# A two-layer hybrid decoder: column tiles that take in a new input together, one table for eight PSUM banks, residual adds on VectorE

## The reference

```python
hn = _rmsnorm(h, g_mix_pre) * valid
u = hn @ w_in                      # 1024 -> 7704 columns, feeds four token mixers and the merge gates
y_sb, y_gla, y_ml, y_ret = ...     # stick-breaking attention, GLA, mLSTM, retention; 256 wide each
merged = sum_n sigmoid(merge_n + b_n) * (y_n @ w_branch[n])
h = h + _rmsnorm(merged @ w_out, g_mix_post)
f = _rmsnorm(h, g_ffn_pre)
h = h + _rmsnorm((silu(f @ ffn_w_gate) * (f @ ffn_w_up)) @ ffn_w_down, g_ffn_post)
```

## Time and profile before

| | |
|---|---|
| median of 3 runs | 1026.15 us (1025.69 to 1026.33) |
| the profiled execution | 1025.4 us |
| its span in the profile | 1023.6 us, 19877 instructions |
| mean granted TensorE clock | 0.992 of full speed |
| HBM read | 154.50 MB, 152 GB/s over the span |
| weights cut on VectorE (L1282) | 355.3 us busy, x290 |
| weights cut on ScalarE (L976) | 302.0 us busy, x290 |

### The profile page before, as it was taken

The page is one execution under the profiler, slowest core; times in us unless marked ns, Lnnn a source line. Parts: engine busy times, 40 slices in busy tenths (PEclk is TensorE's granted clock), DMA queues, the critical chain, the costliest instruction groups (busy, mean ns, idle before and its releaser), DMA issues.

```text
span 1023.6 us, 19877 instructions
## 1 busy us (share of the span) xinstructions
PE 998.8 (98%) x7744; PEld 941.0 (92%) x7744; DVE 600.5 (59%) x843; ACT 518.1 (51%) x825; POOL 152.1 (15%) x140
## 2 busy tenths in 40 slices
PE   7999999999999999999989999999999999999998
PEld 5999888899997999999969998888999899999996
DVE  8556564357956555554465565743679466656443
ACT  5443754465466444544345537544755555454442
POOL 2000000002623121210030000000034321222011
PEclk8999999999999999999999999999999999999998
DMA  5864433335562555555526543343465535555551
GB/s 157 281 214 147 132 94 124 116 109 147 170 195 74 179 164 167 180 176 185 150 67 198 173 142 112 119 124 124 125 165 165 164 124 180 189 180 189 186 185 41
DMA packets 168521, 156.40 MB, mean 153 GB/s; under 512 B 9091, under 2 KB 167022, under 8 KB 168078
## 3 DMA queue, kind: packets, MB, share of 16 engines
q1 hardware_dynamic: 167598, 152.13, 47.9%
q10 hardware_dynamic: 672, 3.37, 1.0%
q0 software_dynamic: 192, 0.07, 0.0%
HBM read 154.50 MB, written 1.05 MB: 152 GB/s over the span
## 4 chain that ended last, share of the span: by engine, by line
PE 88%; DVE 7%; ACT 2%; DMA 2%; issue 1%; SPq 1%; ACTq 0%; DVEq 0%
PE banks L588 27%; PE banks L590 26%; PE banks L589 26%; DVE sub L1300 2%; DMA raw<-in_w_in 2%; DVE sq L1291 1%; PE banks L801 1%; PE banks L803 1%; PE banks L613 1%; DVE lo L1282 1%; ACT hi L976 1%; PE banks L829 1%; PE banks L837 1%; DVE xl L1315 0%; PE banks L767 0%
## 5 line engine op out<-in xcount | busy, mean ns | idle before, releaser
L588 PE MATMUL banks<-xh,hi 128*128 128x272 f32 (+1 forms) x1680 | 490.9, 292 | 9.7 <-DVE xl L1315 4.8
L590 PE MATMUL banks<-xh,lo 128*128 128x272 f32 (+1 forms) x1680 | 480.9, 286 | 0.0
L589 PE MATMUL banks<-xl,hi 128*128 128x272 f32 (+1 forms) x1680 | 479.4, 285 | 0.0
L1282 DVE TENSOR_TENSOR lo<-raw,hi 128x1024 fp32r<-128x1024 f32 (+1 forms) x290 | 355.3, 1228 | 175.1 <-ACT hi L976 173.9
L976 ACT ACTIVATE hi<-raw 128x1024 fp32r<-128x1024 f32 (+1 forms) x290 | 302.0, 1042 | 95.4 <-PE banks L590 55.0
L588 PEld LDWEIGHTS banks<-xh,hi 128*128 128x128 f32 x1680 | 316.4, 188 | 22.8 <-issue 7.8
L589 PEld LDWEIGHTS banks<-xl,hi 128*128 128x128 f32 x1680 | 316.4, 188 | 0.9
L590 PEld LDWEIGHTS banks<-xh,lo 128*128 128x128 f32 x1680 | 316.6, 188 | 0.0
L1664 POOL TENSOR_TENSOR half<-term 128x544 f32<-128x544 f32 (+1 forms) x14 | 31.3, 2238 | 467.9 <-DVE term L1537 467.9
L590 PE MATMUL banks<-ah,lo 128*128 128x272 f32 (+1 forms) x352 | 100.4, 285 | 0.0
L588 PE MATMUL banks<-ah,hi 128*128 128x272 f32 (+1 forms) x352 | 100.1, 284 | 0.0
(11 more groups left out here) (238 smaller groups left out, 1101.7 us busy)
## 6 DMA issues: line engine op xcount, KB each, us to landing
raw<-in_w_in SPq DMA_DIRECT2D x54, 1024.0 KB, 5.2
raw<-in_ffn_w_gate SPq DMA_DIRECT2D x22, 1024.0 KB, 5.3
raw<-in_ffn_w_up SPq DMA_DIRECT2D x22, 1024.0 KB, 5.3
raw<-in_ffn_w_down SPq DMA_DIRECT2D x16, 1024.0 KB, 4.9
raw<-in_w_out SPq DMA_DIRECT2D x8, 1024.0 KB, 5.0
raw<-in_w_in SPq DMA_DIRECT2D x12, 512.0 KB, 4.4
raw<-in_w_branch SPq DMA_DIRECT2D x12, 512.0 KB, 5.5
raw<-in_ffn_w_down SPq DMA_DIRECT2D x8, 768.0 KB, 4.2
```

The source lines that it names most:

```text
L588: mm(dst, wh, mh, start=start, stop=False)
L589: mm(dst, wh, ml, start=False, stop=False)
L590: return mm(dst, wl, mh, start=False, stop=stop)
L1282: tt(lo[g % 2][:, 0:k, c:c + P], raw[g % 2][:, 0:k, c:c + P], hi[g % 2][:, 0:k, c:c + P].bitcast(F32), ALU.subtract).then_inc(lo_ready, 2 ...
```

## The change

- **Together.** A new `together` walks two or three column tiles over the k-tiles in an order given as a list of (tile, k-tile), each tile in a bank of its own; what a k-tile needs (`high_ready`, `low_ready`) is waited for once, the high part before the first matmul and the low part before the third. It is used for `small` and both tiles of `mqk0` (step `first`; lags in k-tiles between them 0, 3, 6 in layer 0 and 0, 0, 3 in layer 1), for the first two tiles of `output` (k-tiles 0 to 5 of both, then 6 and 7), and for the first three of `gate_up`, with the mean of norm 2 beside them.
- **Banks.** `plan_tiles` gives each tile a bank out of eight and a use number (`PLACE`); `bank_free` has one semaphore for each bank. The mixer's tiles still turn between two banks; `output`, `gate_up` and `down` turn in four. The loop of `output` is written out.
- **No dummy matmuls** but the four at the start.
- **VectorE alone** adds the sub-layers (`add_sublayer`: multiply by rstd, add to `hT`, and behind norm 1 `xl`, interleaved by k-tile); the gain is applied by ScalarE in `take_sublayer`. VectorE also makes all of `xl` in `pre_norm`, interleaved with the scaled k-tiles, and in layer 0 with the low parts of halves 0, 2 and 3; half 4 follows.
- **Weights earlier.** The halves of group `mqk1` change places (`SWAPPED`), so its first half lies where `small` has no columns and needn't wait for it. `gate` goes behind `mqk1`. In layer 1, half 3 is cut before the squares and before `pre_norm`; the fourth half of `gate_up` is cut on VectorE within `add_sublayer`. `root(l, 1)` goes ahead of a `round_half` on ScalarE.
- **Start.** ScalarE squares x by tokens with a running sum (`square_first`), right after x has landed and beside the transposes, scales an identity by the sums, and TensorE spreads them over the partitions with three matmuls (`mean_square_first`).

The core of the diff:

```diff
-WARM_START, WARM_PRE, WARM_POST = 4, 6, 8
+RING, NORM_BANK = (0, 1, 2, 3), 5
+FIRST_BANKS, MQK1_BANKS, FFN_BANKS, OUT_BANKS = (0, 1, 7), (4, 0), (4, 6, 7, 3), (4, 6, 7, 1)
+FIRST_LAGS = ((0, 3, 6), (0, 0, 3))
+OUT_ORDER = [(n, k) for n in range(2) for k in range(KT - 2)] + [(n, k) for k in (KT - 2, KT - 1) for n in range(2)]
...
+            def together(tiles, order, mh, ml, q0, high_ready, low_ready, beside=None):
+                open_at, seen = {}, -1
+                for n, k in order:
+                    t, g, c = tiles[n]
+                    if k == 0:
+                        open_at[n] = use_half(g, c), open_tile(t)
+                    (wh, wl), ps = open_at[n]
+                    f, dst = half_cols(g, c), ps[:, 0:T - q0]
+                    if k > seen:
+                        high_ready(k)
+                    mm(dst, wh[:, k, f], mh[:, k, q0:], start=k == 0, stop=False)
+                    mm(dst, wl[:, k, f], mh[:, k, q0:], start=False, stop=False)
+                    if k > seen:
+                        low_ready(k)
+                    last = mm(dst, wh[:, k, f], ml[:, k, q0:], start=False, stop=k == KT - 1)
...
             def output(l):
-                with pe.Fori(0, NOUT // 2) as i:
-                    for j in range(2):
-                        for c in range(2):
-                            features(t + 2 * j + c, g + j, c, gathered_h, gathered_l, q0, i, 2, merged_ready if j + c == 0 else None)
+                together([(t, g, 0), (t + 1, g, 1)], OUT_ORDER, gathered_h, gathered_l, q0, ...)
+                pe.wait_ge(branch_free[l], 2 * KT)
+                for m in range(2, KT):
+                    features(t + m, g + m // 2, m % 2, gathered_h, gathered_l, q0)
             def gate_up(l):
+                together([(t, g, 0), (t + 1, g, 1), (t + 2, g + 1, 0)], in_step((0, 0, 0)), xh, xl, q0, ..., mean_square(l, 2, q0))
+                features(t + 3, g + 1, 1, xh, xl, q0)
...
-                keep_warm(WARM_PRE)
-                pe.wait_ge(branch_free[l], 2 * KT)
-                keep_warm(WARM_POST)
-                keep_warm(WARM_POST - 1)
...
+            def square_first():
+                ss, spare = sq[:, KT - 1, 0:3], (sub[:, 0:4, 0:256], sub[:, 4:8, 0:256])
+                act.wait_ge(meta_loaded, 16)
+                fn(spare[0][0:META], xt[0:META, 0, :]..., ACT.Square, accum_out=ss[0:META, 0:1]).then_inc(ss_ready, 1)
+                act.wait_ge(x_loaded[0], 16)
+                act.wait_ge(x_loaded[1], 16)
+                for b in range(1, 3):
+                    fn(spare[b % 2], xt[:, b, :]..., ACT.Square, accum_out=ss[:, b:b + 1]).then_inc(ss_ready, 1)
+                for b, n in enumerate((META, P, P)):
+                    fn(sq[0:n, b, 0:n], cut["ident"][0:n, 0:n], ACT.Copy, scale=ss[0:n, b:b + 1]).then_inc(ss_ready, 1)
...
             def pre_norm(l):
+                for k in range(KT + 1):
+                    if k < KT:
+                        stt(sq[:, k, :], hT[:, k, :], par[...], rstd[:], ALU.mult, ALU.mult).then_inc(xn_ready[l], 1)
+                    if l == 0 and k == 1:
+                        rest_of_half(0)
+                    if k:
+                        dve.wait_ge(xh_ready[l], k)
+                        tt(xl[:, k - 1, :], sq[:, k - 1, :], xh[:, k - 1, :].bitcast(F32), ALU.subtract).then_inc(xl_ready[l], 1)
+                    if l == 0 and k in (2, 5):
+                        rest_of_half(k // 2 + 1)
+                rest_of_half(2 * G_MIX[l] + ROUND_AHEAD)
+            def add_sublayer(l, n, q0, behind=None):
+                dve.wait_ge(rstd_ready[l], n + 1)
+                for k in range(KT + 2):
+                    if k < KT:
+                        tt(sub[:, k, q0:], sub[:, k, q0:], rstd[:, q0:], ALU.mult).then_inc(post_scaled[l], 1)
+                    if 0 < k <= KT:
+                        dve.wait_ge(post_scaled[l], n // 2 * KT + k)
+                        tt(hT[:, k - 1, q0:], hT[:, k - 1, q0:], sub[:, k - 1, q0:], ALU.add).then_inc(h_ready[l], 1)
+                    if k > 1 and behind:
+                        behind(k - 2)
...
             def gate_up(l):    # VectorE, in the loop
+                    for c in range(2):
+                        dve.wait_ge(al_ready[l], c + 1 + i * 2)
+                        gate_tile(c, t + 4 + c, i, 4)
```

More of the change, by code:

```diff
@@ L21 @@
+import itertools
 from contextlib import ExitStack
@@ L254, in last_of @@
         signal.append(("half", halves, used))
-    free(KT + DEPTH)
+        put(bank)
+    free(*RING, *RING, *RING[:DEPTH])
     for _ in range(DEPTH):
         f = {}
+        turn = itertools.cycle(RING[:2])
         def stage(name):
             f[name] = len(signal)
-        stage("norm0"), free(1)
+        stage("norm0"), free(NORM_BANK)
         for step in STEPS:
             stage(step)
-            if step[0] == "group":
-                kind = KIND[step[1]]
-                if kind == "two":
-                    last_of(1), last_of(1)
-                else:
-                    last_of(2)
+            if step[0] == "first":
+                stage(("group", "small")), last_of(FIRST_BANKS[0], 2)
+                stage(("group", "mqk0")), [last_of(bank) for bank in FIRST_BANKS[1:]]
+            elif step == ("group", "mqk1"):
+                [last_of(bank) for bank in MQK1_BANKS]
+                next(turn)
+            elif step[0] == "group":
+                last_of(next(turn)), last_of(next(turn))
             elif step[0] == "logit":
-                last_of(1)
+                last_of(next(turn))
             elif step[0] == "branch":
@@ L445, in build, with half_cols @@
         G_END = GROUPS * DEPTH
+        SWAPPED = [g + MIX_NO["mqk1"] for g in G_MIX]
+        def half_cols(g, c):
+            c = 1 - c if g in SWAPPED else c
+            return slice(c * P, c * P + P)
         def group_k(g):
@@ L456, in wait_tile, with bank_of, uses_of @@
             eng.wait_ge(tile_done if kind == "tile" else half_used, n + i * per)
+        def bank_of(t):
+            return banks[:, PLACE[t][0], :]
+        def uses_of(t, step):
+            bank, n = PLACE[t]
+            if not step:
+                return bank_free[bank], n, 0
+            assert PLACE[t + step][0] == bank and n > 0
+            return bank_free[bank], n, PLACE[t + step][1] - n
         def wait_taken(eng, t, i=0, step=0):
-            eng.wait_ge(bank_free[t % 2], t // 2 + 1 + i * (step // 2))
+            free, n, per = uses_of(t, step)
+            eng.wait_ge(free, n + 1 + i * per)
         def group_tile(l, name):
@@ L621, in mean_square, with tile @@
+            def mean_square(l, n, q0):
                 t = TILE[l][f"norm{n}"]
                 ps = open_tile(t)
-                if n == 0 and l == 0:
-                    pe.wait_ge(sq_first, KT - 1)
-                    close_tile(mm(ps[:, 0:T], cut["mean"], sq[:, 0, :], start=True, stop=True), t)
-                elif n == 0:
+                def tile(k):
+                    pe.wait_ge(sq_ready[l][n], k + 1)
+                    last = mm(ps[:, 0:T - q0], cut["mean"], sq[:, k, q0:], start=k == 0, stop=k == KT - 1)
+                    if k == KT - 1:
+                        close_tile(last, t)
+                if n == 2:
+                    return tile
+                if n == 0:
@@ new lines, in mean_square, with mean_square_first, first @@
+                    tile(KT - 1)
+            def mean_square_first():
+                t = TILE[0]["norm0"]
+                ps = open_tile(t)
+                pe.wait_ge(ss_ready, 6)
+                for b, (at, n) in enumerate(((0, META), (KB1, P), (KB2, P))):
+                    last = mm(ps[:, at:at + n], cut["mean"][0:n, :], sq[0:n, b, 0:n], start=True, stop=True)
+                close_tile(last, t)
+            def first(l):
+                g, t = G_MIX[l], group_tile(l, "small")
+                assert MIX_NO["small"] == 0 and MIX_NO["mqk0"] == 1 and group_tile(l, "mqk0") == t + 1
+                together([(t, g, 0), (t + 1, g + 1, 0), (t + 2, g + 1, 1)], in_step(FIRST_LAGS[l]), xh, xl, 0,
+                         lambda k: pe.wait_ge(xh_ready[l], k + 1), lambda k: pe.wait_ge(xl_ready[l], k + 1))
@@ L1002, in root @@
+            def root(l, n, q0):
+                t = TILE[l][f"norm{n}"]
+                wait_tile(act, t)
+                taken(fn(rstd[:, q0:], bank_of(t)[:, 0:T - q0], ACT.Ln, bias=cut["eps"]), t)
+                wait_taken(act, t)
                 fn(rstd[:, q0:], rstd[:, q0:], ACT.Exp, scale=-0.5).then_inc(rstd_ready[l], 1)
@@ L1036, in group @@
                     taken(ins, t + j)
-                    round_half(half + j)
-                if kind == "small":
-                    round_half(half + 1)
+                    if name != "mqk1":
+                        round_half(half + j)
+                    elif j:
+                        round_half(half)
+                        round_half(half + 1)
             def logit(l, j):
```

415 lines of the change are left out of this document (203 added, 212 removed).

## The result

The change takes **1014.75 us** (median of 5 runs, 1014.18 to 1018.97), the kernel before 1026.15 beside it (5 runs, 1024.15 to 1026.95): ratio 0.9898, interval 0.9882 to 0.9915. A second measurement of the change, unaltered, gives 0.9882 (0.9865 to 0.9900), so the saving is 10.5 to 12 us (11.4 and 12.0 by the medians, 10.5 and 12.1 by the ratios), of 18.1 forecast. There are two profiled executions of it, with spans of 1012.6 and 1013.9 us, against 1023.6 before.

A forecast was written before the change was run, and what follows sets the result against it. The prediction took TensorE as dense inside stages, so only seven seams, waiting on chains through other engines, could gain: 2.4 + 2.0 + 4.05 + 3.3 + 5.2 + 1.15 = 18.1 us off 1025.4, median 1008.0, range 1004.5 to 1015.

The forecast's parts named there:

- a half clock in the windows of the seams: At the three seams: the prediction's stated sign of being wrong; full clock there was its sign of being right.
- Paces: Seams: VectorE's adds start 0.35 us apart, three-input instructions 0.43; TensorE takes 1.59 us a k-tile at gate and up.
- Merge to output, 1.0 each: Merge to output projection, both layers: two tiles going together cover waits for late k-tiles, gain 1.0 us each, 2.0 in all.
- Layer 0 to 1, 5.2: Seam between layers: faster scaling and adding, three tiles together ending at 538.2, gain 5.2 us.
- Output to gate and up, 4.05 and 3.3: Output projection to gate and up: fifth tile starts sooner, gain 4.05 us in layer 0 and 3.3 in layer 1.
- half 4's wait: Gate and up: the fifth tile waits for weight half 4, until 326.35 us in layer 0 and 830.75 in layer 1.
- The low end of the range: Whole kernel: 1004.5 us, if half 4 is not late after all (1.7) and the start is better by 1.8.
- The step that failed: Seams inside: the clock stays full without dummies, though TensorE idles 2.0 to 2.7 us at each of three.
- the clock falls where the dummies were: Rival, three inside seams: half clock costs 2.25 us each, 1015 us in all; chance 0.20.
- the start: Start of layer 0: VectorE begins at 13.1 us, the gate is done at 35.5; gain 2.4 us.
- End, 1.15: End of the kernel: VectorE's interleaved scalings and adds finish at 1017.9 in place of 1019.09, gain 1.15 us.
- Slower, through the wait for low parts in the loops: Rival, feed-forward loops: VectorE holds gate tiles back for low parts; 1048 us at 0.5 us a tile; chance 0.03.

The follow-up runs named there:

- the one with the late weights: Eight dummies at the start in place of four, against the kernel with seam dummies and half 4 cut before the third root and table load: 0.9805 of the kernel before.
- the dummies' experiment: The change with fewer dummy matmuls than before put back at the seams (3 and 4, 5, 5), against the kernel before: 0.9834.
- the profile in which the transposes kept full pace: The change with dummies back at the seams and half 4 cut before the third root and table load, against the kernel before: 0.9801, 1005.1 us.

## Why the prediction was wrong in size

The direction held, and so did the mechanism at full clock; 18.1 us were forecast and 11.4 came. The forecast named a half clock in the windows of the seams as the sign of being wrong, and that sign is there. By its own steps:

- **Paces.** A k-tile's 1.59 us of TensorE: measured 1.59. VectorE's 0.35 start to start: at the end L1405 and L1408 alternate 0.34 apart with a duration of 0.42. The Trainium skill ("VectorE: DVE Perf Modes", section "The DRAIN you can't avoid") says that the next instruction waits for the pipeline to empty, and in the same paragraph that one which is not held starts earlier; the forecast took only the first half. These rows show instructions that overlap by 0.08 us, so the row decided rightly, and it fits the second half.
- **Merge to output, 1.0 each** (1.5 with VectorE's earlier start): measured 1.46 in layer 0, and in layer 1 2.98 less the 1.53 of the dip in the profile of before, in every profile in which the tiles go together but the one with the late weights. Right.
- **Layer 0 to 1, 5.2**: 4.9 wherever the clock held behind the norm, with VectorE adding; 2.9 and 1.8 where it didn't. The step was right at full clock.
- **Output to gate and up, 4.05 and 3.3**: 2.5 and 2.1 of the stretches' 3.6 and 2.8 at full clock. The mis-sized term is half 4's wait: 0.8 and 1.0 were forecast, holes of 1.26 and 1.43 came, and taking it away gave 1.4 and 1.5. The low end of the range priced the whole of it at 1.7; it was worth 2.95. From the first scaling to the fifth tile 18.5 us were forecast in layer 0 and 19.2 came. Another 0.35 of layer 0's 4.05 was a misreading: VectorE takes the fourth tile at 330.34, and the forecast let TensorE begin the fifth at 330.4, where it had begun it at 330.05:

```profile
330.05 0.29 PE L588 MATMUL banks<-xh,hi 128*128 128x272 f32 x1
```

  In layer 1 the same step was done rightly (834.34 to 834.05). With both, a tenth of a microsecond of layer 0's stretch stays unexplained.
- **The step that failed**: that the clock holds. The forecast said against its rival that "at 530 to 536 it was busy for 4.24 of 6 us by modelled ends, with idle gaps of half a microsecond, and stayed at full". That window of the kernel before begins where its dummies end:

```profile
528.00 2.91 PE L569 MATMUL banks<-ones 128*128 128x272 f32 x12
```

  So the row showed sparse work behind dummies, and the change has none; without the dummies the same kernel shows a mean of 0.57 at 530 to 538, above. The rival "the clock falls where the dummies were" had 0.20 and 1015 us, and that is what happened, at 4.9 us by the dummies' experiment and 7 by the rival's price. That 1014.75 came so near its 1015 is luck: the rival's price was 2 us too high, and the longer wait for half 4, the misreading and the start helped to make up for it. At the start the forecast counted the means at half pace but not the transposes ahead of them, which, with x landing later, moved VectorE's start from 13.1 to 16.3; in the profile in which the transposes kept full pace VectorE began at 13.0, and the start gained 2.45 where 2.4 was forecast.
- **End, 1.15**: 1.1, with the clock at half there (0.51), and -0.3 in the second profile, by its slower stores. Right.
- **Slower, through the wait for low parts in the loops**: no hole over 0.3 us stands in either layer's loops. Right to be left at 0.03.

With dummies, and with half 4's wait of 0.8 and 1.0 taken away, the terms give 18.1 + 1.8 = 19.9 us; measured 20.4 (0.9801 of 1026.15). Some of that agreement is luck: by stretches the profile gains 20.7, of which 1.5 is the dip in the profile of before, and its start is among the two best. Still, no stretch of it is over 0.6 us from its terms once the dip is left out, so the parts were right for a kernel that keeps its clock, and the change doesn't.

What stays open is what decides, from one execution to the next, at which seam and in which transposes the clock falls. Two executions of the same kernel differed, and no run here shows the cause.

## What to carry to other kernels

A dummy that is worth nothing in one order of the work was worth 5 us in the next: price the clock by how full TensorE will be behind the seam, not by what the dummies bring today. When several tiles go through arriving input together, the operand loads behind them come due sooner by as much as is won; look there for the next wait, and cut them in a gap that is already idle. On a queue in order, count what a step leaves on the busy engine (eight float32 matmuls) before counting what it takes off the idle one.
